# Reading the moving operand backwards, with high and low weights interleaved, in a hybrid encoder step

## The chip, the cores and the metric

The kernel runs on one core of one Trainium2 chip. The metric is the device time of that core in microseconds (us). The kernel before took 2157.94 us, the median of three runs (2157.59 to 2158.12).

## The reference

One inference step of a two-layer trunk in float32, on 1024 prompt frames and 32 sample frames of width 1024:

```python
def trunk(x, b_conv, b_h, c_conv, p):
    for l in range(DEPTH):                      # DEPTH = 2
        hn = rmsnorm(x, p['norm_mix_pre'][l])
        if l % 2 == 0:                          # gMLP spatial gating || RG-LRU, one in and one out projection
            m, v, bc, bh = mixer_even(hn, ...)  # 1024 -> 2048, 1024 -> 1024
        else:                                   # gated short convolution
            m, cc = mixer_odd(hn, ...)          # 1024 -> 3072, 1024 -> 1024
        x = x + rmsnorm(m, p['norm_mix_post'][l])
        hn = rmsnorm(x, p['norm_ffn_pre'][l])
        f = jnp.square(jax.nn.relu(hn @ p['mlp_up'][l])) @ p['mlp_down'][l]   # 1024 -> 4096 -> 1024
        x = x + rmsnorm(f, p['norm_ffn_post'][l])
```

Nearly all the arithmetic is in the projections. Everything else (norms, gates, convolutions, the scan) works on the 1056 x 1024 activations between them.

## The kernel before, in words

**Layout.** Channels lie on the 128 partitions and tokens along the free dimension. The 1056 tokens are cut into three tiles t = 0, 1, 2 of 352, and the 1024 channels into eight chunks k. Each activation is kept as a sum of two float32r tensors, a rounded high part and the low remainder: `x_hi`, `x_lo` for the residual stream's normed input, `h_hi`, `h_lo` for the inner activation. A chunk of x takes 4608 bytes in a partition and its tiles begin 1536 bytes apart. A chunk of h takes 4352 bytes and its tiles begin 1408 bytes apart.

**Products.** A *unit* is one 128-column panel of a weight matrix times one token tile. For each of the eight chunks k it issues three float32r matmuls of 128x128 by 128x352, high weights by high data (L698), high weights by low data (L699), low weights by high data (L700), and all 24 accumulate into one PSUM bank. There are 552 units; the first four are issued in another order (L716, L720, L729). Units rotate over six PSUM banks, so a unit may begin when the unit six before it has been read out.

**Weights.** A panel (512 KB) arrives by a DMA on SyncE's queue as raw float32. ScalarE writes the rounded high part (`high`, L876), VectorE writes the low part as raw minus high (`low`, L1183), and each raises a semaphore that the next engine waits for. 166 of the panels after the first four, and three of the first four, go to three *rotating places* p0, p1, p2. Each place is 8192 bytes of `w_all`: 4096 bytes of high weights, then 4096 of low weights, chunk after chunk of 512 bytes, and the raw weights land where the low ones will be written (`w_all_raw` is a second name of the same bytes). The other panels go to the place `s` in h, `x` in the gaps of `x_hi`, and `ha`, `hb` in h.

**Where things lie.** The tensors are laid one after another in a partition. `x_hi`, `x_lo`, `h_hi`, `h_lo` and `f` have sizes that are multiples of 1024 bytes; then 128 bytes are skipped, and `w_all` begins. So every chunk in a rotating place begins 128 bytes past a multiple of 512, counted from the start of `x_hi`. Tiles of x begin at multiples of 512; tiles 0 and 2 of h begin at multiples of 256, and tile 1 of h begins 128 bytes past a multiple of 256.

**Order.** The order on every engine is written out by hand. ScalarE's `high` of a panel stands at most six units before the panel's first use and VectorE's `low` one unit later. They stand among the reading out of PSUM (`evacuate`), the squares, the splits into high and low, and, between blocks, the norms, residual sums and splits of the new x. At the start, VectorE rounds the first half of the first panel (L1341), splits the first four chunks of x (L1248) and makes four low halves (L1330), each of 512 columns.

Of the kernel before, what the change touches and what calls it, by code (L numbers as in the profile page):

```python
# [13 lines left out]
P = 128  # L14
D = 1024
# [7 lines left out]
KC = D // P  # L23
# [27 lines left out]
F32 = mybir.dt.float32  # L51
F32R = mybir.dt.float32r
# [6 lines left out]
EVEN_COLS = [8, 9, 10, 11, 4, 5, 6, 7, 12, 13, 14, 15, 0, 1, 2, 3]  # L59
EVEN_KINDS = ["xb"] * 4 + ["v"] * 4 + ["gb"] * 4 + ["u"] * 4  # L60
ROTATING = ("p0", "p1", "p2")


def plan():
# [4 lines left out]
    units, loads, starts, outs, ups = [], [], [], [], []  # L69
    freed = {s: None for s in ROTATING}  # L70

    def oldest():
        return min(ROTATING, key=lambda s: -1 if freed[s] is None else freed[s])

# [19 lines left out]
    def tile_block(panels, src, slots):  # L94
        ls = []
        for (name, row, col, kind, m), (slot, free) in zip(panels, slots):
            if slot is None:
                slot = min((s for s in ROTATING if s not in [loads[l][3] for l in ls]),
                           key=lambda s: -1 if freed[s] is None else freed[s])
# [63 lines left out]
def build(nc, A, O):  # L163
# [27 lines left out]
    with ExitStack() as ctx:  # L191
        at_byte = [nc.sbuf_base + (-nc.sbuf_base) % 32]

        def place(name, shape, dt, offset=None):
            size = 4
            for n in shape[1:]:
                size *= n
            here = at_byte[0] if offset is None else offset
            if offset is None:
                at_byte[0] += size + (-size) % 32  # L200
            return nc.alloc_sbuf_tensor_at(name, shape, dt, offset=here)
# [6 lines left out]
        x_hi = place("x_hi", [P, KC * XS], F32R)  # L208
        at_x_lo = at_byte[0]
        x_lo = place("x_lo", [P, KC * XS], F32R)  # L210
# [6 lines left out]

        at_byte[0] += 128
        at_w = at_byte[0]
        w_all = place("w_all", [P, 6, D], F32R)  # L220
        w_all_raw = place("w_all_raw", [P, 6, D], F32, at_w)
        at_tmp = at_byte[0]
        tmp = [place(f"tmp{t}", [P, TT], F32) for t in range(3)]
        rstd = place("rstd", [P, TOK], F32)
# [64 lines left out]
        def tile_at(buf, t):  # L289
            return t * (TT + QUAD if buf.shape[1] == KC * XS else TT)  # L290

        def pt(buf, c, t):
            c0 = c * (buf.shape[1] // KC) + tile_at(buf, t)
            return buf[:, c0:c0 + TT]

        def part(buf, k0, k1, t, c0=0, c1=TT):
            return tiles3(buf)[:, k0:k1, tile_at(buf, t) + c0:tile_at(buf, t) + c1]
# [11 lines left out]
        def w_views(slot, l):  # L309
            if slot in ROTATING:  # L310
                s = ROTATING.index(slot)
                three = [w[:, i, :].rearrange("p (k n) -> p k n", k=KC)
                         for w, i in ((w_all, 2 * s), (w_all, 2 * s + 1), (w_all_raw, 2 * s + 1))]
            elif slot == "s":
                three = [w[:, i, :].rearrange("p (k n) -> p k n", k=KC)
                         for w, i in ((w_s, 0), (w_s, 1), (w_s_raw, 1))]
            elif slot == "x":
                three = [part(w, 0, KC, 2, c, c + P) for w, c in ((x_hi, 32), (x_hi, 32 + P), (x_hi_raw, 32 + P))]
            else:
                t = ("ha", "hb").index(slot)  # L320
                c = (32, 0)[t]
                if LOADS[l].first == START[2] + t:
                    three = [part(w, k, k + 4, t, c, c + 2 * P) for w, k in ((h_hi, 4), (h_hi, 0), (h_hi_raw, 0))]
                else:
                    three = [part(w, 4, 8, t, c, c + 2 * P) for w in (h_hi, h_lo, h_lo_raw)]
            return three

        W = [w_views(l.slot, i) for i, l in enumerate(LOADS)]

        def w_k(l, which, k):  # L330
            v = W[l][which]
            if LOADS[l].slot in ("ha", "hb"):
                return v[:, k // 2, (k % 2) * P:(k % 2) * P + P]
            return v[:, k, :]


        SLOTS = ROTATING + ("s", "x", "ha", "hb")
        fill = [sum(LOADS[j].slot == l.slot for j in range(i)) for i, l in enumerate(LOADS)]
# [5 lines left out]
        def bank(n):  # L344
            return ps[:, n % NB, 0:TT]
# [329 lines left out]
        def _(pe):  # L675
            EVEN_ORDER = (4, 5, 6, 7, 0, 1, 2, 3)
            IN_ORDER = tuple(range(KC))

            def unit(n):
                u = UNITS[n]  # L680
                X = u.src == "X"
                src = (x_hi, x_lo) if X else (h_hi, h_lo)
                order = EVEN_ORDER if u.kind == "eo" else IN_ORDER
                l, t = u.load, u.t
                pe.wait_ge(w_ready, l + 1)
                if n >= NB:
                    by_scalar = UNITS[n - NB].kind in SCALAR_OUT
                    pe.wait_ge(evac_a if by_scalar else evac_d, evac_no[n - NB] + 1)
                phase = START.index(max(s for s in START if s <= n))
                dst = bank(n)  # L690
                for i, k in enumerate(order):
                    if X and n - START[phase] in (0, 4, 8):
                        pe.wait_ge(x_ready, 24 * phase + 8 * t + k + 1)
                    if u.m == 0:
                        h_part(n, i)
                    hi, lo = pt(src[0], k, t), pt(src[1], k, t)
                    wh, wl = w_k(l, 0, k), w_k(l, 1, k)
                    nc.tensor.matmul(dst, wh, hi, start=(i == 0), stop=False)  # L698
                    nc.tensor.matmul(dst, wh, lo, start=False, stop=False)  # L699
                    last = nc.tensor.matmul(dst, wl, hi, start=False, stop=(i == KC - 1))  # L700
                    if i == KC - 1:
                        last.then_inc(pe_unit, 1)
                    between(n, i)

            def first_high(n, h):

                if h == 1:
                    pe.wait_ge(w_high, n + 1)
                elif n == 0:
                    pe.wait_ge(w_half, 1)  # L710
                else:
                    pe.wait_ge(w_halves, n)
                for k in range(4 * h, 4 * h + 4):
                    if n == 0:
                        pe.wait_ge(x_high, k + 1)
                    nc.tensor.matmul(bank(n), w_k(n, 0, k), pt(x_hi, k, 0), start=(k == 0), stop=False)  # L716
                for k in range(4 * h, 4 * h + 4):
                    if n == 0:
                        pe.wait_ge(x_ready, k + 1)
                    nc.tensor.matmul(bank(n), w_k(n, 0, k), pt(x_lo, k, 0), start=False, stop=False)  # L720

            def first_low(n, h):

                if h == 0:
                    pe.wait_ge(w_low, n + 1)
                else:
                    pe.wait_ge(w_ready, n + 1)
                for k in range(4 * h, 4 * h + 4):
                    last = nc.tensor.matmul(bank(n), w_k(n, 1, k), pt(x_hi, k, 0), start=False, stop=(k == KC - 1))  # L729
                if h == 1:  # L730
                    last.then_inc(pe_unit, 1)

            def h_part(n, i):

                kind, t = UNITS[n].kind, UNITS[n].t
                if kind in ("dn0", "dn", "dn3"):
                    done = index[n - 1 - t] + 1
                    if i == 0 and t == 0:
                        pe.wait_ge(h_ready, done - 3)
                    if i == KC - 1:  # L740
                        pe.wait_ge(h_ready, done - 2 + t)
                if kind == "oo":
                    if i == 0 and t == 0:
                        pe.wait_ge(y_ready, 21)
                    if i == KC - 1:
                        pe.wait_ge(y_ready, 22 + t)
                if kind == "eo":
                    if i == 0 and t == 0:
                        pe.wait_ge(mix_a, 12)
                    if i == 4 and t == 0:  # L750
                        pe.wait_ge(mix_a, 21)
                    if i == KC - 1:
                        pe.wait_ge(mix_a, 22 + t)
# [76 lines left out]
            def between(n, i):  # L830

                if n < START[1]:
                    if (n, i) in GATE_AT:
                        gate(*GATE_AT[n, i])
                    if (n, i) in VALUE_AT:
                        values_to_rows(*VALUE_AT[n, i])
                    if (n, i) in SPATIAL_AT:
                        spatial(SPATIAL_AT[n, i])
                if (n, i) in COL_AT:
                    col_sums(*COL_AT[n, i])  # L840
# [5 lines left out]
            for i, (n, h) in enumerate(turns):  # L846
                first_high(n, h)
                if i > 0:
                    first_low(*turns[i - 1])
            first_low(3, 1)  # L850
            for n in range(4, N_UNITS):
                unit(n)

            last = N_UNITS - 1
# [5 lines left out]
            n = NORM[3, "post", 2]  # L860
# [823 lines left out]
```

## Time and profile before

| | before |
|---|---|
| device time, median of three | 2157.94 us |
| span of the profiled execution, first to last instruction | 2155.1 us |
| device time of the profiled execution itself | not recorded beside its span |
| mean granted TensorE clock | 0.999 |
| matmuls (PE) busy | 2146.0 us, 100%, 13496 instructions |
| weight loads (PEld) busy | 2135.0 us, 99%, 13496 instructions |
| VectorE (DVE) busy | 908.0 us, 42% |
| ScalarE (ACT) busy | 652.9 us, 30% |
| GpSimd (POOL) busy | 100.1 us, 5% |
| DMA queues | 138.65 MB, mean 64 GB/s |

The times of a matmul and of a weight load in the profile include what overlaps the next one: matmuls are shown at about 322 ns although one begins every 158 ns or so. What counts for throughput is the distance from start to start. The median run stands 2.8 us above the profiled span; that is what lies around the span, and it is taken as constant.

### The profile page before, as it was taken

The numbers are of one execution on the slowest core, as the hardware profiler recorded it, in microseconds if no ns is written. First come the engines' busy times: TensorE is split into PE (matmuls) and PEld (weight loads), VectorE is DVE, ScalarE is ACT, GpSimd is POOL, SyncE is SP. The second block draws the span as 40 slices with busy tenths as digits, with TensorE's granted clock in tenths as the row PEclk, the third lists the DMA queues.
The fourth block names the chain that finished last, engine by engine and source line by source line (L and its number), as shares of the span: only waits on it lengthen the run. The fifth ranks groups of instructions, "written<-read, shape, count | busy, mean of one in ns | idle before, by whom it ended". The sixth has DMA issues, their size and how long they took to land.

```text
span 2155.1 us, 31488 instructions
## 1 busy us (share of the span) xinstructions
PE 2146.0 (100%) x13496; PEld 2135.0 (99%) x13496; DVE 908.0 (42%) x1414; ACT 652.9 (30%) x1105; POOL 100.1 (5%) x127
## 2 busy tenths in 40 slices
PE   9999999999999999999999999999999999999998
PEld 9999999999999999999999999999999999999998
DVE  8766367323322322334953333493223223322336
ACT  6673355202301310333511112453013103202332
POOL 2000000000000000000043231000000000000000
PEclk9999999999999999999999999999999999999999
DMA  5111422111111111141311114222111111111142
GB/s 165 35 41 40 139 88 72 50 40 49 50 42 47 49 50 40 49 135 44 120 50 47 43 50 139 67 84 59 42 48 50 49 40 50 50 42 48 50 140 81
DMA packets 208410, 138.65 MB, mean 64 GB/s; under 512 B 6000, under 2 KB 204784, under 8 KB 208272
## 3 DMA queue, kind: packets, MB, share of 16 engines
q1 hardware_dynamic: 207552, 135.51, 20.6%
q8 instruction: 107, 1.75, 0.3%
q10 hardware_dynamic: 720, 1.13, 0.1%
q14 instruction: 31, 0.25, 0.0%
HBM read 119.22 MB, written 17.40 MB: 63 GB/s over the span
## 4 chain that ended last, share of the span: by engine, by line
PE 99%; ACT 1%; DMA 0%; DVE 0%; issue 0%; DVEq 0%; ACTq 0%
PE ps L698 32%; PE ps L700 32%; PE ps L699 32%; PE ps L773 1%; PE ps L801 0%; PE ps L729 0%; PE ps L720 0%; DMA w_all_raw<-in_w_in_even_dram 0%; PE ps L716 0%; PE ps L784 0%; PE ps L760 0%; ACT L1074 0%; ACT L1030 0%; ACT lru L1030 0%; ACT lru L1032 0%; ACT gelu L1074 0%
## 5 line engine op out<-in xcount | busy, mean ns | idle before, releaser
L698 PE MATMUL ps<-x_hi,w_all 128*128 128x352 f32 x2304 | 747.0, 324 | 0.0
L700 PE MATMUL ps<-x_hi,w_all 128*128 128x352 f32 x2304 | 739.1, 321 | 0.0
L699 PE MATMUL ps<-x_lo,w_all 128*128 128x352 f32 x2304 | 739.1, 321 | 0.0
L698 PE MATMUL ps<-h_hi,w_all 128*128 128x352 f32 x1728 | 556.2, 322 | 0.0
L700 PE MATMUL ps<-h_hi,w_all 128*128 128x352 f32 x1728 | 555.2, 321 | 0.0
L699 PE MATMUL ps<-h_lo,w_all 128*128 128x352 f32 x1728 | 555.2, 321 | 0.0
L698 PEld LDWEIGHTS ps<-x_hi,w_all 128*128 128x128 f32 x2304 | 432.4, 188 | 2.7
L699 PEld LDWEIGHTS ps<-x_lo,w_all 128*128 128x128 f32 x2304 | 432.4, 188 | 2.2
L700 PEld LDWEIGHTS ps<-x_hi,w_all 128*128 128x128 f32 x2304 | 432.3, 188 | 0.0
L876 ACT CAST w_all<-w_all_raw 128x1024 fp32r<-128x1024 f32 x166 | 173.5, 1045 | 525.1 <-DMA w_all_raw<-in_mlp_down_dram 324.8
L698 PEld LDWEIGHTS ps<-h_hi,w_all 128*128 128x128 f32 x1728 | 324.5, 188 | 0.3 <-DVE h_lo L1452 0.3
L699 PEld LDWEIGHTS ps<-h_lo,w_all 128*128 128x128 f32 x1728 | 324.5, 188 | 0.0
L700 PEld LDWEIGHTS ps<-h_hi,w_all 128*128 128x128 f32 x1728 | 324.4, 188 | 0.0
L1286 DVE SCALAR_TENSOR_TENSOR tmp<-ps,rstd 128x352 f32<-128x352 f32 x192 | 100.3, 523 | 419.2 <-PE ps L700 419.0
L937 ACT ACTIVATE tmp<-tmp 128x352 f32<-128x352 f32 x192 | 95.7, 498 | 472.4 <-DVE tmp L1286 472.2
L1292 DVE TENSOR_TENSOR f<-ps,f 128x352 f32<-128x352 f32 x144 | 75.3, 523 | 358.6 <-PE ps L700 358.6
L1183 DVE TENSOR_TENSOR w_all<-w_all_raw,w_all 128x1024 fp32r<-128x1024 f32 x166 | 201.8, 1216 | 17.2 <-ACT w_all L876 17.2
L1266 DVE TENSOR_TENSOR h_lo<-tmp,h_hi 128x352 fp32r<-128x352 f32 x192 | 98.9, 515 | 2.3 <-ACT h_hi L939 2.3
L939 ACT CAST h_hi<-tmp 128x352 fp32r<-128x352 f32 x192 | 93.7, 488 | 6.1
L1289 DVE COPY f<-ps 128x352 f32<-128x352 f32 x48 | 25.2, 525 | 138.0 <-PE ps L700 138.0
L698 PE MATMUL ps<-h_hi,x_hi 128*128 128x352 f32 x192 | 61.7, 321 | 0.0
L700 PE MATMUL ps<-h_hi,x_hi 128*128 128x352 f32 x192 | 61.7, 321 | 0.0
(201 smaller groups left out, 1416.0 us busy)
## 6 DMA issues: line engine op xcount, KB each, us to landing
w_all_raw<-in_mlp_up_dram SPq DMA_DIRECT2D x60, 512.0 KB, 3.9
w_all_raw<-in_mlp_down_dram SPq DMA_DIRECT2D x60, 512.0 KB, 3.8
x_save<-f SPq DMA_DIRECT2D x9, 1408.0 KB, 6.0
x_old<-x_save SPq DMA_DIRECT2D x9, 1408.0 KB, 11.5
w_all_raw<-in_c_w_in_dram SPq DMA_DIRECT2D x22, 512.0 KB, 3.7
w_all_raw<-in_w_in_even_dram SPq DMA_DIRECT2D x12, 512.0 KB, 3.6
x_old<-in_x_cols_dram SPq DMA_DIRECT2D x3, 1408.0 KB, 12.8
w_all_raw<-in_w_out_even_dram SPq DMA_DIRECT2D x6, 512.0 KB, 3.8
```

The source lines that it names most:

```text
L698: nc.tensor.matmul(dst, wh, hi, start=(i == 0), stop=False)
L699: nc.tensor.matmul(dst, wh, lo, start=False, stop=False)
L700: last = nc.tensor.matmul(dst, wl, hi, start=False, stop=(i == KC - 1))
L773: nc.tensor.matmul(ps[:, M0, 0:LT], gate_w[:, g, j, :], xc[j % 2][:, t * LT:(t + 1) * LT], start=True, stop=True).then_inc(gate_pe, 1)
L876: nc.scalar.copy(W[l][0], W[l][2]).then_inc(w_high, 1)
L937: nc.scalar.activation(tmp[n % 3][:, :], tmp[n % 3][:, :], ACT.Square).then_inc(h_sq, 1)
L939: nc.scalar.copy(pt(h_hi, u.m, u.t), tmp[n % 3][:, :]).then_inc(h_high, 1)
L1183: nc.vector.tensor_tensor(lo, raw, hi.bitcast(F32), ALU.subtract).then_inc(w_ready, 1)
L1266: nc.vector.tensor_tensor(pt(h_lo, u.m, u.t), tmp[n % 3][:, :], pt(h_hi, u.m, u.t).bitcast(F32), ALU.subtract).then_inc(h_ready, 1)
L1286: ins = nc.vector.scalar_tensor_tensor(tmp[n % 3][:, :], bank(n), 0.0, scale, ALU.max, ALU.mult)
L1289: ins = nc.vector.tensor_copy(pt(f, m, t), bank(n))
L1292: ins = nc.vector.tensor_tensor(pt(f, m, t), bank(n), pt(f, m, t), ALU.add)
```

## The change

All the projection matmuls now go through a helper `product`, which gives the moving operand and the result in reversed column order: the last of the 352 columns is read and written first. The result lies in PSUM as before.

In the rotating places the high and the low weights of a column lie side by side (4 bytes of high, 4 of low), so a chunk of 128 columns takes 1024 bytes and one weight load reads every second word. The three places begin at 0, 8192 and 16384 bytes, moved further by 0, 16 and 96 bytes. Raw weights have a tensor of their own, `w_raw`, of 3 x 4096 bytes. To make room, the DMA scratch reservation is set to 2048 bytes, which moves all tensors in a partition together. The places `s`, `x`, `ha`, `hb` keep their layout. No wait, queue or order is changed.

```diff
+W_SHIFT = (0, 4, 24)
+WS = len(ROTATING) * 2 * D + 32
...
-        w_all = place("w_all", [P, 6, D], F32R)
-        w_all_raw = place("w_all_raw", [P, 6, D], F32, at_w)
+        w_all = place("w_all", [P, WS], F32R)
+        w_raw = place("w_raw", [P, len(ROTATING), D], F32)
...
             if slot in ROTATING:
                 s = ROTATING.index(slot)
-                three = [w[:, i, :].rearrange("p (k n) -> p k n", k=KC)
-                         for w, i in ((w_all, 2 * s), (w_all, 2 * s + 1), (w_all_raw, 2 * s + 1))]
+                at = s * 2 * D + W_SHIFT[s]
+                pairs = w_all[:, at:at + 2 * D].rearrange("p (k n two) -> p two k n", two=2, n=P)
+                three = [pairs[:, 0], pairs[:, 1], w_raw[:, s, :].rearrange("p (k n) -> p k n", k=KC)]
...
+            def product(out, w, x, start, stop):
+
+                return nc.tensor.matmul(out[:, ::-1], w, x[:, ::-1], start=start, stop=stop)
...
-                    nc.tensor.matmul(dst, wh, hi, start=(i == 0), stop=False)
-                    nc.tensor.matmul(dst, wh, lo, start=False, stop=False)
-                    last = nc.tensor.matmul(dst, wl, hi, start=False, stop=(i == KC - 1))
+                    product(dst, wh, hi, i == 0, False)
+                    product(dst, wh, lo, False, False)
+                    last = product(dst, wl, hi, False, i == KC - 1)
...
-    nc = _bacc.Bacc("TRN2", target_bir_lowering=False, num_devices=1)
+    nc = _bacc.Bacc("TRN2", target_bir_lowering=False, num_devices=1, dynamic_dma_scratch_size=2048)
```

The matmuls of the first four units are changed in the same way.

## Rows read from the trace of the kernel before

**Rows 1.** The page: busy time by engine, granted clock, shares of the ending chain

```profile
PE 2146.0 (100%) x13496; PEld 2135.0 (99%) x13496; DVE 908.0 (42%) x1414; ACT 652.9 (30%) x1105; POOL 100.1 (5%) x127
...
PEclk9999999999999999999999999999999999999999
...
PE 99%; ACT 1%; DMA 0%; DVE 0%; issue 0%; DVEq 0%; ACTq 0%
```

**Rows 2.** Groups: line, engine, operation, tensors, shape, count | busy, mean ns | idle before

```profile
L698 PE MATMUL ps<-x_hi,w_all 128*128 128x352 f32 x2304 | 747.0, 324 | 0.0
L698 PE MATMUL ps<-h_hi,w_all 128*128 128x352 f32 x1728 | 556.2, 322 | 0.0
...
L876 ACT CAST w_all<-w_all_raw 128x1024 fp32r<-128x1024 f32 x166 | 173.5, 1045 | 525.1 <-DMA w_all_raw<-in_mlp_down_dram 324.8
L1183 DVE TENSOR_TENSOR w_all<-w_all_raw,w_all 128x1024 fp32r<-128x1024 f32 x166 | 201.8, 1216 | 17.2 <-ACT w_all L876 17.2
L1398 DVE TENSOR_TENSOR_SCAN mixed<-lru,lru 128x1024 f32<-128x1024 f32 x4 | 9.2, 2292 | 0.4
```

**Rows 3.** Busy time in stretches: stretch, its length, each engine's busy time (instructions)

```profile
0.00:50.00 50.00, 48.26 (x275) 45.36 (x276) 40.54 (x71) 30.71 (x48) 12.35 (x39) 1.00 0.53 172
500.00:1000.00 500.00, 500.00 (x3155) 500.00 (x3154) 156.22 (x261) 126.65 (x213) 0.00 (x0) 1.00 0.19 56
```

**Rows 4.** Timeline, TensorE, three matmuls in a row: start us, length us

```profile
1000.40 0.32 PE L698 MATMUL ps<-h_hi,w_all 128*128 128x352 f32 x1
1000.56 0.32 PE L699 MATMUL ps<-h_lo,w_all 128*128 128x352 f32 x1
1000.71 0.32 PE L700 MATMUL ps<-h_hi,w_all 128*128 128x352 f32 x1
```

**Rows 5.** Timeline, TensorE: first matmuls of units on h's tiles 0, 1, 2, 0

```profile
598.74 0.32 PE L698 MATMUL ps<-h_hi,w_all 128*128 128x352 f32 x1
...
602.54 0.32 PE L698 MATMUL ps<-h_hi,w_all 128*128 128x352 f32 x1
...
606.38 0.32 PE L698 MATMUL ps<-h_hi,w_all 128*128 128x352 f32 x1
...
610.18 0.32 PE L698 MATMUL ps<-h_hi,w_all 128*128 128x352 f32 x1
```

**Rows 6.** Timeline, TensorE: float32 passes of 352 columns before the first unit

```profile
4.35 0.76 PE L810 MATMUL ps<-rstd 128*128 128x352 f32 x2
...
5.54 0.46 PE L810 MATMUL ps<-rstd 128*128 128x352 f32 x1
```

**Rows 7.** Timeline, matmuls and weight loads after a wait, next load not held back

```profile
6.33 0.43 PE L716 MATMUL ps<-x_hi,w_all 128*128 128x352 f32 x1 [0.33 <-DVE w_all L1341]
...
6.44 0.19 PEld L716 LDWEIGHTS ps<-x_hi,w_all 128*128 128x128 f32 x1
...
6.59 0.53 PE L716 MATMUL ps<-x_hi,w_all 128*128 128x352 f32 x2
```

**Rows 8.** Timeline, the same after a wait, next load held back

```profile
8.31 0.42 PE L720 MATMUL ps<-x_lo,w_all 128*128 128x352 f32 x1
...
8.56 0.19 PEld L716 LDWEIGHTS ps<-x_hi,w_all 128*128 128x128 f32 x1
...
8.57 0.42 PE L716 MATMUL ps<-x_hi,w_all 128*128 128x352 f32 x1
```

**Rows 9.** Timeline, a product while a 32-column weight load runs

```profile
83.92 0.32 PE L700 MATMUL ps<-x_hi,w_all 128*128 128x352 f32 x1
...
83.92 0.10 PEld L787 LDWEIGHTS ps<-ident,gelu 128*32 128x32 f32 x1
...
84.08 0.27 PE L787 MATMUL ps<-ident,gelu 128*32 128x128 f32 x1
```

**Rows 10.** Timeline, a low panel of VectorE and the unit that uses it

```profile
1054.24 1.18 DVE L1183 TENSOR_TENSOR w_all<-w_all_raw,w_all 128x1024 fp32r<-128x1024 f32 x1
...
1056.60 0.32 PE L698 MATMUL ps<-x_hi,w_all 128*128 128x352 f32 x1
```

**Rows 11.** Timeline, VectorE at the start

```profile
5.85 0.43 DVE L1341 CAST w_all<-w_all_raw 128x512 fp32r<-128x512 f32 x1 [4.62 <-DMA w_all_raw<-in_w_in_even_dram]
6.19 2.06 DVE L1248 SCALAR_TENSOR_TENSOR x_lo<-f,vecs,x_hi 128x352 fp32r<-128x352 f32 x4
```

More of the change, by code:

```diff
@@ L715, in first_high @@
                         pe.wait_ge(x_high, k + 1)
-                    nc.tensor.matmul(bank(n), w_k(n, 0, k), pt(x_hi, k, 0), start=(k == 0), stop=False)
+                    product(bank(n), w_k(n, 0, k), pt(x_hi, k, 0), k == 0, False)
                 for k in range(4 * h, 4 * h + 4):
@@ L719, in first_high @@
                         pe.wait_ge(x_ready, k + 1)
-                    nc.tensor.matmul(bank(n), w_k(n, 0, k), pt(x_lo, k, 0), start=False, stop=False)
+                    product(bank(n), w_k(n, 0, k), pt(x_lo, k, 0), False, False)
             def first_low(n, h):
@@ L728, in first_low @@
                 for k in range(4 * h, 4 * h + 4):
-                    last = nc.tensor.matmul(bank(n), w_k(n, 1, k), pt(x_hi, k, 0), start=False, stop=(k == KC - 1))
+                    last = product(bank(n), w_k(n, 1, k), pt(x_hi, k, 0), False, k == KC - 1)
                 if h == 1:
```

## The prediction

> **What bounds the kernel now.** I read the page first, then the groups, then stretches of busy time, then the timeline at single instructions. The page says that TensorE is busy over the whole span, at the full of its two clock levels (2.4 GHz) in every slice, and the chain that ended last is 99% TensorE [rows 1]. No other engine is near it: VectorE 42%, ScalarE 30%. So only two things can move the time: the distance between matmul starts, or a new wait of TensorE.
>
> The groups show what the matmuls are: products of 128x352 in float32r, of which 4 x 24 belong to the first units and 548 x 24 = 13,152 to the rest, 13,248 in all. Those with weights in `w_all` are 3 x (2304 + 1728) = 12,096 on L698 to L700 [rows 2], and 3 x 24 = 72 in the first units, so 12,168 read a rotating place and 1,080 another one. The busy mean of 322 ns is no cost, since matmuls overlap; the stretch from 500 to 1000 us gives the cost: 3155 starts in 500.00 us, 158.5 ns each [rows 3]. At 2.4 GHz, 352 columns at one a cycle are 146.7 ns. So 11.8 ns of each matmul, 7.4%, is not columns, and 12,168 x 11.8 ns = 144 us is all that the change could ever reach.
>
> How much of that is unavoidable? The nearest row is a float32 pass of 352 columns, at two cycles a column: four of them begin in 5.54 - 4.35 = 1.19 us, about 297 ns each where the columns take 293.3 [rows 6]. That leaves some 3 to 4 ns between passes, and a float32r product would stand at about 150 ns with no more loss than that. 158.5 has some 8.5 ns more.
>
> Does this excess depend on addresses? A unit of 24 matmuls on h's tile 0 takes 602.54 - 598.74 = 3.80 us, on tile 1 3.84, on tile 2 3.80 [rows 5]: 158.3, 160.0, 158.3 ns a matmul with the same weights. From the layout, weights of a rotating place and tile 1 begin at the same place modulo 256 bytes, and the other tiles 128 bytes apart. So reading weights and reading moving data do disturb each other by address, and 1.7 ns of it shows. Singly, starts stand 0.16 and then 0.15 us apart [rows 4]: the disturbance varies from one matmul to the next, and the short ones are near 155 ns.
>
> Does it come from the weight load at all? After a wait the next load starts 6.44 - 6.33 = 0.11 us later, once the first has been read, and the second product starts 0.15 us after that, at 0.26 [rows 7]. In the other case the next load is held back until 8.56, when the product before it is practically over, and the distance is again 8.57 - 8.31 = 0.26 us [rows 8]. And where only 32 columns of weights are loaded beside a product, it takes 84.08 - 83.92 = 0.16 us [rows 9]. Within the 10 ns of these rows, a product without a weight load beside it is hardly shorter. This speaks against the load as the cause of all 8.5 ns, and for a cost of the float32r stream itself.
>
> **The change part by part.** *Reversed moving columns and results.* No row of before reads or writes backwards. Lower bound: it takes away the whole excess, 150 ns a product. Upper bound: backwards runs at the rate of the float32 passes, 297 ns. I take no cost and no gain by itself, since 352 columns backwards touch the same words.
>
> A rule of the Trainium skill speaks against this part: "PSUM — Partial Sum Buffer", section Specifications, says that any non-contiguous access pattern slows matmuls significantly, because PSUM's lines are 8 bytes. A step of -1 has the same pairs in the other order; if it counted as non-contiguous, the rule would put the kernel with the backwards rival below, towards its far end of 3990 us. No trace here shows which holds.
>
> *Weights side by side.* A load now reads every second word, so it walks 8 bytes for each weight, twice as far as before. In 0.11 us the load walks 1024 bytes, and the moving stream, at 352 x 4 bytes in 147 ns, walks 1024 bytes in 107 ns: both now move at the same pace. No row shows in which order the load takes its columns. If it is last to first, the two now walk side by side and keep their distance, where before they crossed; if it is first to last, they cross faster than before. With a kept distance, each product should look like the undisturbed ones. For these I take the short distance of the timeline, 155 ns [rows 4], between no change (158.5) and the bound of 150. That is 3.5 ns x 12,168 = 43 us less. The 1,080 products of other places I leave as they are; at 3.5 ns they would add at most 4 us. The offsets of 16 and 96 bytes decide where the kept distance lies: if it is bad, tile 1's row says what that costs, 160 ns, or +1.5 x 12,168 = +18 us.
>
> *ScalarE's and VectorE's panels.* `high` now writes, and `low` reads and writes, every second word: 166 x 1045 ns and 166 x 1216 ns today [rows 2]. No row has a step of two. Bounds: no change, or the slowest VectorE group of 1024 columns, 2292 ns, that is +1.08 us each, +179 us of VectorE in all; ScalarE's bound is the same sum, at most +179 us. Neither is on the chain: 908 + 179 is 50% of the span, and readouts have six banks of 3.8 us each. What they can hit are the tight places between blocks. At 1054.24 a `low` ends at 1055.42 and its unit starts at 1056.60, 1.2 us later [rows 10]; behind that instruction on VectorE the readouts and the squares' sums queue. Two such panels in a row at +0.8 each (nearer the upper end, since every stream but one is strided) would be 0.4 us late. The trace has about six such places with 1.2 to 2.3 us to spare, so 0 to 6 us, and I take 2.
>
> The Trainium skill's "Vector Engine (DVE) Microarchitecture Reference", section 5.2, measured streams without adjacent pairs at about 1.7 to 2.5 ns a column against 1.05. By that, 1024 columns would gain 0.7 to 1.5 us each, and the 2 us would become up to 6 or 8. No row here shows it.
>
> *The start.* L1341 (0.43 us for 512 columns) is on the path, and the four splits behind it too [rows 11]. A strided write may cost 0 to 0.5 us there; I take 0.5. The four low halves behind have 1.9 us per turn of TensorE.
>
> *Raw weights apart, scratch.* Nothing: the same DMAs to another place behind the same waits; 64 GB/s is far from a bound, and the scratch only moves everything together.
>
> **Sum.** Against the profiled execution: 2155.1 - 43 + 2 + 0.5 = 2114.6 us of span. The median of the runs is 2.8 us above the span, so 2157.9 - 40.5 = 2117 us.
>
> **The rivals.**
> *The whole excess goes.* The 8.5 ns are all crossing of the two streams. For it: the excess depends on addresses, and float32 passes at half the pace lose only 3 to 4 ns. Against: the held-back and the 32-column load [rows 8, 9]. 8.5 x 12,168 = 103 us, plus the 2.5: 2057 us.
> *It does nothing.* The excess is the stream's own, and the 1.7 ns of tile 1 moves from one tile to another: 2153 to 2162 us. For it: rows 7 against 8.
> *Slower by place or feed.* The streams now lie as on tile 1 at all times (+18 us), or `low` at 2.3 us makes units wait; it decides once the delay of two panels passes 1.2 us: 2165 to 2180 us.
> *Slower by backwards reading or writing.* Each product pays for the reversed order. At 1 ns a product it would be +13 us; at the full bound, 297 ns, +138.5 x 13,248 = +1835 us, 3990 us. It decides from 3.5 ns a product up. For it only that TensorE's stream has no slack; against it that every word is touched once, as before.
>
> **How the numbers follow.** My forecast, 10 to 70 us saved, has 0.33; the whole excess 0.20; a small gain of 4 to 10 us 0.10; nothing 0.13; slower by place or feed 0.10; slower by backwards access 0.14. Faster: 0.63, same (within 0.2%, 4.3 us, about what a measurement of this kernel can tell) 0.13, slower 0.24. The range goes from 2045, below the whole-excess case with the other places' 4 us and a margin for its 150 ns, up to 2178, which takes in the case of place and feed. Left out are most of the backwards case and little below. The likeliest case's own range is 2088 to 2148.
>
> **What would show it.** In the stretch from 500 to 1000 us the count of matmuls should rise from 3155 to about 3225 (150 ns: 3333; 160 ns: 3125). Units on tile 1 should be as long as on tiles 0 and 2, except where an offset differs; units of p0, p1 and p2 may differ from one another. `low` should be longer than 1216 ns, `high` than 1045, with a few tenths of idle TensorE at block boundaries. TensorE stays busy 99%. I am wrong if the distance is unchanged, if matmuls at all places lengthen alike (backwards access), or if TensorE's idle time before L698 grows to tens of us.

## The result, and the profile after

| | before | after |
|---|---|---|
| device time, median | 2158.03 us (4 runs, 2157.59 to 2159.05) | 2176.68 us (4 runs, 2176.47 to 2176.76) |
| ratio to before, 95% interval | | 1.0086 (1.0072 to 1.0100) |
| span of the profiled execution | 2155.1 us | 2174.9 us |
| busy VectorE, ScalarE | 908.0, 652.9 us | 913.8, 673.2 us |

The kernel after is 18.7 us, 0.86%, slower. Faster was forecast (2117 us). The forecast's range went up to 2178 us only to take in the rival of place and feed; that the measured time lies just inside it is luck, since neither turned out to be the cause.

The busy times of the kernel after:

```profile
PE 2166.4 (100%) x13496; PEld 2155.5 (99%) x13496; DVE 913.8 (42%) x1414; ACT 673.2 (31%) x1105; POOL 95.0 (4%) x127
```

The middle stretch of the kernel after, columns as in [rows 3]; the 1.00 behind the busy times is the granted clock:

```profile
500.00:1000.00 500.00, 500.00 (x3124) 500.00 (x3123) 153.05 (x255) 128.17 (x206) 0.00 (x0) 1.00 0.20 57
```

TensorE is as busy as before at the same clock, 1.00 of 2.4 GHz [rows 1, 3]: no new wait, more time in each product. 3124 starts in 500 us are 160.1 ns a product, against 3155 and 158.5 [rows 3]. All projections now go through one line, L684. The timeline of the kernel after shows the units on h's tiles 0 and 1. Each row begins with the last product of the unit before, so 24 products lie between one row and the next:

```profile
603.21 0.48 PE L684 MATMUL ps<-h_hi,w_all 128*128 128x352 f32 x2
...
607.05 0.48 PE L684 MATMUL ps<-h_hi,w_all 128*128 128x352 f32 x2
...
610.94 0.49 PE L684 MATMUL ps<-h_hi,w_all 128*128 128x352 f32 x2
```

3.84 and 3.89 us for tiles 0 and 1, where it was 3.80 and 3.84 [rows 5]. These are units of p2, whose tile 1 of h is the one bad case left among the rotating places. Over the 548 units after the first four, the starts in the two traces lie 2120.8 and 2140.4 us apart, first to last. That is 19.6 of the span's 19.8 us; the rest is the start. (The medians differ by 1.1 us less than the spans, since the profiled execution of before has its span 2.9 us below the median, that of after 1.8.)

The groups of the kernel after, weight loads of a rotating place and of another one, then the two panel operations:

```profile
L684 PEld LDWEIGHTS ps<-h_hi,w_all 128*128 128x128 f32 x3456 | 613.4, 194 | 0.3 <-DVE h_lo L1459 0.3
L684 PEld LDWEIGHTS ps<-h_hi,x_hi 128*128 128x128 f32 x384 | 67.4, 188 | 0.0
...
L883 ACT CAST w_all<-w_raw 128x1024 fp32r<-128x1024 f32 x166 | 193.7, 1167 | 531.3 <-DMA w_raw<-in_mlp_down_dram 325.3 <-DMA w_raw<-in_mlp_up_dram 124.9 <-DMA w_raw<-in_c_w_in_dram 59.8
...
L1190 DVE TENSOR_TENSOR w_all<-w_raw,w_all 128x1024 fp32r<-128x1024 f32 x166 | 207.2, 1248 | 18.8 <-ACT w_all L883 18.8
```

`high` is the rounding to the high part on ScalarE, `low` the subtraction on VectorE. A load with a step of two is shown 6 ns longer (194 against 188). `high` grew from 1045 to 1167 ns, `low` only from 1216 to 1248 [rows 2].

### The profile page after: what moved, and what is told of

Read it like the earlier page. It is cut to its first block, busy times and chain, and to the rows that moved or that the text cites. A ratio compares the mean times of both kernels' runs of the same rounds, so it can differ in the third digit from the quotient of the medians.

```text
span 2174.9 us, 31488 instructions
## 1 busy us (share of the span) xinstructions
PE 2166.4 (100%) x13496; PEld 2155.5 (99%) x13496; DVE 913.8 (42%) x1414; ACT 673.2 (31%) x1105; POOL 95.0 (4%) x127
## 4 chain that ended last, share of the span: by engine, by line
PE 60%; issue 38%; POOL 0%; DVE 0%; DMA 0%; ACT 0%; DVEq 0%; ACTq 0%; POOLq 0%
PE ps L684 59%; PE ps L780 1%; PE ps L808 0%; DMA w_raw<-in_w_in_even_dram 0%; PE ps L791 0%; DVE cy L1510 0%; POOL cy L664 0%; POOL h_lo L667 0%; DVE x_lo L1255 0%; POOL row_rstd L673 0%; PE ps L767 0%; ACT h_hi L1154 0%; DVE x_old L1633 0%; PE ps L812 0%; DVEq L193 0%
## 5 line engine op out<-in xcount | busy, mean ns | idle before, releaser
L684 PE MATMUL ps<-x_hi,w_all 128*128 128x352 f32 x4656 | 1133.7, 326 | 0.0
L684 PE MATMUL ps<-h_hi,w_all 128*128 128x352 f32 x3456 | 837.2, 324 | 0.0
L684 PEld LDWEIGHTS ps<-x_hi,w_all 128*128 128x128 f32 x4656 | 825.4, 194 | 3.1 <-ACT w_all L992 0.2
L684 PE MATMUL ps<-x_lo,w_all 128*128 128x352 f32 x2328 | 751.7, 324 | 0.1
L684 PEld LDWEIGHTS ps<-h_hi,w_all 128*128 128x128 f32 x3456 | 613.4, 194 | 0.3 <-DVE h_lo L1459 0.3
L684 PE MATMUL ps<-h_lo,w_all 128*128 128x352 f32 x1728 | 559.5, 324 | 0.0
L684 PEld LDWEIGHTS ps<-x_lo,w_all 128*128 128x128 f32 x2328 | 450.7, 194 | 2.5 <-DVE x_lo L1255 0.3
L883 ACT CAST w_all<-w_raw 128x1024 fp32r<-128x1024 f32 x166 | 193.7, 1167 | 531.3 <-DMA w_raw<-in_mlp_down_dram 325.3
L684 PEld LDWEIGHTS ps<-h_lo,w_all 128*128 128x128 f32 x1728 | 335.7, 194 | 0.0
L1190 DVE TENSOR_TENSOR w_all<-w_raw,w_all 128x1024 fp32r<-128x1024 f32 x166 | 207.2, 1248 | 18.8 <-ACT w_all L883 18.8
L684 PE MATMUL ps<-h_hi,x_hi 128*128 128x352 f32 x384 | 95.3, 325 | 0.0
L684 PEld LDWEIGHTS ps<-h_hi,x_hi 128*128 128x128 f32 x384 | 67.4, 188 | 0.0
L684 PE MATMUL ps<-h_lo,x_hi 128*128 128x352 f32 x192 | 62.3, 325 | 0.0
L1268 DVE TENSOR_TENSOR x_hi_raw<-x_hi_raw,tmp 128x352 f32<-128x352 f32 x56 | 29.2, 521 | 68.4 <-ACT tmp L937 67.5
```

What stands on the lines that cost most here:

```text
L684: return nc.tensor.matmul(out[:, ::-1], w, x[:, ::-1], start=start, stop=stop)
L883: nc.scalar.copy(W[l][0], W[l][2]).then_inc(w_high, 1)
L1190: nc.vector.tensor_tensor(lo, raw, hi.bitcast(F32), ALU.subtract).then_inc(w_ready, 1)
L1268: nc.vector.tensor_tensor(dst, dst, sq, ALU.add).then_inc(f_acc, 1)
```

## The experiments

In this table the last six columns are the mean distance from one product's start to the next, in ns, worked out from the starts of all products in each trace: the rotating places, chunks two to seven of each unit, by the source (x or h) and its tile. Distances of over 175 ns, where a short matmul of another kind lies between or is just over, are left out. Ratios have 95% intervals; a time without one is a single run (before: four).

| kernel | us | ratio to before | x 0 | x 1 | x 2 | h 0 | h 1 | h 2 |
|---|---|---|---|---|---|---|---|---|
| before | 2158.0 | | 158.4 | 158.6 | 158.6 | 158.4 | 160.0 | 158.4 |
| after | 2176.7 | 1.0086 (1.0072 to 1.0100) | 160.0 | 160.0 | 160.0 | 160.0 | 160.7 | 160.0 |
| e1 reversed only | 2187.1 | 1.0134 (1.0117 to 1.0151) | 161.0 | 161.0 | 161.0 | 160.1 | 162.2 | 160.2 |
| e2 interleaved only | 2185.4 | 1.0127 (1.0112 to 1.0142) | 160.8 | 160.8 | 160.9 | 161.3 | 161.1 | 160.8 |
| e3 after, no shift | 2175.4 | 1.0079 (1.0064 to 1.0094) | 160.0 | 160.0 | 160.0 | 160.0 | 160.0 | 160.0 |
| e4 after, result forward | 2176.6 | | 160.0 | 160.0 | 160.0 | 160.0 | 160.7 | 160.0 |
| e5 reversed, moved | 2182.9 | | 160.7 | 160.7 | 160.7 | 160.7 | 160.0 | 160.7 |
| e6 after, moved | 2175.5 | | 160.0 | 160.0 | 160.0 | 160.0 | 160.0 | 160.0 |
| f1 forward, moved | 2181.4 | 1.0109 (1.0092 to 1.0126) | 160.7 | 160.7 | 160.7 | 160.7 | 160.0 | 160.8 |
| e8 narrow loads, forward | 2153.1 | | 158.6 | 159.2 | 157.8 | 158.4 | 157.8 | 157.9 |
| e9 narrow, reversed | 2178.7 | | 160.9 | 160.0 | 160.0 | 160.1 | 161.6 | 160.0 |
| e10 narrow, interleaved | 2173.4 | | 160.8 | 159.7 | 159.6 | 160.8 | 159.9 | 159.9 |
| e11 narrow, after | 2174.4 | | 160.0 | 160.0 | 160.0 | 160.0 | 160.1 | 160.0 |
| e7 fewer columns, forward | 2011.5 | | 158.4 | 146.7 | 133.3 | 158.3 | 146.5 | 133.3 |
| e12 fewer columns, after | 2017.9 | | 160.0 | 146.8 | 131.9 | 160.0 | 147.8 | 131.9 |

**e1, e2: each half alone.** In e1 the old layout of the weights stays:

```diff
-                return nc.tensor.matmul(out, w, x, start=start, stop=stop)
+                return nc.tensor.matmul(out[:, ::-1], w, x[:, ::-1], start=start, stop=stop)
```

> The kernel before with only the moving columns and results reversed. If backwards access alone causes the loss: 160.0 ns a product in all places and 2174 to 2178 us. If the interleaved weight loads (194 ns shown against 188) cause it: unchanged, 2156 to 2160 us. If only the two together do (both streams at one pace): 155 to 159 ns here, 2120 to 2160 us.

In e2 the kernel after has that line turned back.

> The kernel after with moving columns and results forward again; interleaved weights stay. Backwards access as the cause: 158.3 ns again, 2157 to 2162 us. Weight loads as the cause: 160 ns in p0, p1, p2 and 158.3 in x, ha, hb, 2172 to 2178 us. The two together as the cause: below 160 ns, 2155 to 2165 us.

The same stretch of e1 and, below it, of e2:

```profile
500.00:1000.00 500.00, 500.00 (x3121) 500.00 (x3120) 151.98 (x255) 122.26 (x205) 0.00 (x0) 1.00 0.19 56
```

```profile
500.00:1000.00 500.00, 500.00 (x3108) 500.00 (x3107) 150.62 (x251) 125.56 (x204) 0.00 (x0) 1.00 0.19 56
```

Neither expectation names this outcome: each half alone costs more than both together, +29.1 and +27.4 us against +18.7. In e2 the loss is nearly all in the rotating places; products from `ha` and `hb`, forward and contiguous there, are at 158.3 ns in the units that no other matmul interrupts. It also differs by rotating place, and the places differ by their shift: on x's tiles p0 has 160.1 ns, p1 160.0 and p2 162.4 to 162.5. In e1 it is everywhere, `ha` and `hb` at 162.2. The 161.0 of e1 on x is a mean of two kinds of units: in each rotating place some 16 units stand at 160.0 ns and 12 to 14 at 162.2, with weights and data at the same addresses.

**e3: the shifts.**

```diff
-W_SHIFT = (0, 4, 24)
+W_SHIFT = (0, 0, 0)
```

> The kernel after with the three places shifted by 0, 0, 0 bytes instead of 0, 16, 96. If the place of the weights decides: p1 and p2 become as p0, the 162.2 ns of p2 on h's tile 1 go to 160.0, 1.3 us less (2175 us). If the shifts had helped p1 and p2: p1, p2 above 160 ns, 2180 us or more.

1.3 us less than after, as the first theory had it, all of it from p2 on h's tile 1. The shifts of 16 and 96 bytes do nothing useful.

**e4: the direction of writing.**

```diff
-                return nc.tensor.matmul(out[:, ::-1], w, x[:, ::-1], start=start, stop=stop)
+                return nc.tensor.matmul(out, w, x[:, ::-1], start=start, stop=stop)
```

> The kernel after with the results written forward while the moving columns are read backwards; the token columns of each tile come out permuted, so the values are not the reference's. If writing PSUM backwards costs anything: 1.5 ns a product less, 2157 us. If only reading decides: 160.0 ns as after, 2176 us.

```profile
500.00:1000.00 500.00, 500.00 (x3124) 500.00 (x3123) 153.06 (x256) 128.15 (x206) 0.00 (x0) 1.00 0.19 57
```

3124 starts, exactly as in the kernel after. Writing PSUM backwards costs nothing that can be seen beside backward reading; what there is comes from reading.

**e5, e6, f1: other places.** e5 is e1 with the places moved by 64, 128, 192 bytes, e6 the kernel after with those shifts, f1 the kernel before with 32, 64, 192 bytes. The core of e5 and f1 (e5's numbers):

```diff
+W_SHIFT = (16, 32, 48)
...
-                         for w, i in ((w_all, 2 * s), (w_all, 2 * s + 1), (w_all_raw, 2 * s + 1))]
+                at = [i * D + W_SHIFT[s] for i in (2 * s, 2 * s + 1)]
+                three = [w[:, c:c + D].rearrange("p (k n) -> p k n", k=KC)
+                         for w, c in ((w_all, at[0]), (w_all, at[1]), (w_all_raw, at[1]))]
```

> Reversed moving columns with contiguous weights, the three places moved by 64, 128, 192 bytes. A tile read backwards begins 1404 bytes later, that is some 128 bytes on modulo 256. If only the place where the two streams meet decides, p1 (moved by 128) returns to 158.3 ns on x's tiles, and 160 on h's tile 1; p0 and p2 lie between. If reading backwards itself costs, every place stays at 160 ns or more, 2175 us or more.

> The kernel after with shifts of 64, 128, 192 bytes instead of 0, 16, 96. If the kept distance of two streams of one pace decides, some place is clear of the other stream and falls to 155 ns or less, another rises above 162. If pairs and backwards reading hold the products at 160.0 whatever the distance, all three places stay within 0.5 ns of 160 on x's tiles, 2174 to 2180 us.

> Forward columns and contiguous weights as before, the three places moved by 32, 64, 192 bytes (160, 192 and 64 past a multiple of 256). If only meeting at one place modulo 256 costs: 158.3 ns for all tiles in p1 and p2, tile 1 of h included, 2 us less than before in all. If the present place is the only good one: 160 ns in p1, p2 also on x, 2165 us or more. If a place can free the product of all disturbance: 155 ns somewhere.

Reversed and contiguous (e5), p0 and p2 stand at 160.0 ns on x and p1, the one that should have come back to 158.3, at 162.2. Backwards, no place that was tried is below 160.0. Forward and contiguous (f1), p1 and p2 have 160.0 ns on every tile, p0 162.0 to 162.3 on all but h's tile 1, where it has 160.0: of the places tried, the one that the kernel before has (128 past a multiple of 256) is the only one at 158.3. The smaller scratch reservation, which f1 has and before has not, is not the cause: in f1 products from place `x`, whose weights did not move, are still at 158.3 ns on h's tiles 0 and 2. Interleaved and reversed (e6), it is 160.0 whatever the place:

```profile
500.00:1000.00 500.00, 500.00 (x3126) 500.00 (x3125) 153.22 (x256) 128.26 (x208) 0.00 (x0) 1.00 0.19 57
```

The place is not the whole story. Two units of f1 take their weights from `ha`, at the same addresses, times tile 2 of x. The first product of each and the first of the next unit:

```profile
345.24 0.33 PE L684 MATMUL ps<-x_hi,h_hi 128*128 128x352 f32 x1
...
349.24 0.33 PE L684 MATMUL ps<-x_hi,h_hi 128*128 128x352 f32 x1
```

```profile
1458.18 0.32 PE L684 MATMUL ps<-x_hi,h_hi 128*128 128x352 f32 x1
...
1461.99 0.32 PE L684 MATMUL ps<-x_hi,h_hi 128*128 128x352 f32 x1
```

4.00 against 3.81 us for the same 24 products. The starts show why: the first unit runs at a steady 166 to 167 ns, the second in the cycle 155, 159, 157 or 158, 161 or 162. f1 falls into the slow rhythm within five products of two short matmuls of the norms, which stand at 320.2 us in the middle of a `hb` unit that had run at 158.3 ns until then. So a stream settles in one of a few rhythms (with full loads of contiguous weights, means such as 158.3, 160.0, 162.2 or 166.7 ns forwards, 160.0 or 162.2 backwards), and how it was entered counts beside the places. What chooses the rhythm was not tested. A mean of the table can be a mixture of such rhythms. In before, two uninterrupted units of the rotating places stand at 166.7 ns.

**e8, e9, e10, e11: hardly any weight load beside the product.** The same edit in four kernels: forward and contiguous (e8), reversed (e9), interleaved (e10), both (e11, shown as e8):

```diff
+            def product(out, w, x, start, stop, t=0):
+                m = P if start or stop else (128, 64, 32)[t]
+                return nc.tensor.matmul(out[0:m], w[:, 0:m], x, start=start, stop=stop)
```

> The kernel before where 22 of 24 products of a unit load 128, 64, 32 weight columns on tiles 0, 1, 2 (on tiles 1 and 2 the upper output channels are summed incompletely). If the excess of 8.5 ns is weight load against moving stream: about 158.3, 154, 151 ns on x's tiles. If it is the stream's own: all within 1 ns of 158.3.

> Reversed columns, contiguous weights, and the narrowed loads of e8 (128, 64, 32 weight columns on tiles 0, 1, 2; upper output channels summed incompletely). Forward, the narrow loads gave 157.9 ns on tile 2. If backwards reading costs by itself: 160 ns or more on tile 2 too. If it costs only by meeting the weight load: about 158 on tile 2, 161 on tile 0.

> Forward columns, interleaved weights, narrowed loads of 128, 64, 32 columns (upper output channels summed incompletely). If the interleaved load disturbs by the lines it reads: the loss of 1.8 to 4 ns shrinks with the number of columns, about 158 ns on tile 2. If each load with a step of two costs a fixed amount: 160 to 162.5 on tile 2 as on tile 0.

> The kernel after with narrowed loads of 128, 64, 32 columns on tiles 0, 1, 2 (upper output channels summed incompletely). If side by side at one pace has already removed what the load disturbs, and 160.0 ns is the backward stream's own distance: 160.0 on all tiles, within 0.3 ns. If a disturbance by the load is still in the 160.0: tile 2 falls to 158 or less.

In e8 loads of 128 columns are shown at 188 ns, of 64 at 134, and those of 32:

```profile
L681 PEld LDWEIGHTS ps<-h_hi,w_all 128*32 128x32 f32 x1008 | 108.8, 108 | 49.4
```

Of 188 ns shown, 80 are gone at 32 columns, and the product hardly gains. The timeline of e8, one unit on h's tile 2 (row to row, 24 products):

```profile
604.82 0.48 PE L681 MATMUL ps<-h_hi,w_all 128*128 128x352 f32 x2
...
608.62 0.48 PE L681 MATMUL ps<-h_hi,w_all 128*128 128x352 f32 x2
```

The same of e9, reversed:

```profile
610.65 0.49 PE L681 MATMUL ps<-h_hi,w_all 128*128 128x352 f32 x2
...
614.49 0.48 PE L681 MATMUL ps<-h_hi,w_all 128*128 128x352 f32 x2
```

The same of e11, reversed and interleaved:

```profile
610.18 0.48 PE L684 MATMUL ps<-h_hi,w_all 128*128 128x352 f32 x2
...
614.02 0.49 PE L684 MATMUL ps<-h_hi,w_all 128*128 128x352 f32 x2
```

3.80, 3.84 and 3.84 us. With a quarter of the load, a forward product takes 157.8 to 157.9 ns, 0.5 to 0.8 less than with all of it (with half of it, x's tile 1 has 159.2, 0.6 more); a backward one 160.0; and the kernel after keeps its 160.0 on every tile. These are no mixtures: with 32 columns loaded, all 151 uninterrupted units of the rotating places on tile 2 stand at 157.7 to 158.0 ns in e8 and at 159.9 to 160.0 in e9. So in the kernel after the load disturbs next to nothing (in p2 on h's tile 1, 162.2 ns becomes 160.2), and 160.0 is the distance of a backward product of 352 columns at the alignments of these tiles. e10 lies between its two theories: on tile 2 of x, p0 has 160.7 (160.1 in e2), p1 158.2 (160.0) and p2 160.0 (162.5). The interleaved load disturbs a forward product, partly by its columns.

**e7, e12: fewer columns.**

```diff
+            def product(out, w, x, start, stop, t=0):
+                n = TT if start or stop else (352, 320, 288)[t]
+                return nc.tensor.matmul(out[:, 0:n], w, x[:, 0:n], start=start, stop=stop)
```

> The kernel before where 22 of 24 products of a unit take 352, 320, 288 columns on tiles 0, 1, 2 (the last columns of tiles 1 and 2 are summed incompletely). Measures what the 11.7 ns above the columns are. A fixed cost of each product: 13.3 ns less for each 32 columns, 158.3, 145.0, 131.7 ns on x's tiles. A share of the stream: 14.4 less, 158.3, 143.9, 129.5. Bound by the weight load: no product under 158.

e12 is the same on the kernel after, with both slices reversed.

> The kernel after where 22 of 24 products take 352, 320, 288 columns on tiles 0, 1, 2, backwards (the last columns of tiles 1 and 2 summed incompletely). Forward, x's tiles gave 158.4, 146.9, 133.7 ns. If reading backwards costs a fixed amount a product: about 160.0, 148.5, 135.4. If it costs by the column: the distance to forward shrinks, to 1.4 at 288. If only the length of 352 is unlucky: 146.7 and 133.3, as forward.

The timelines on h's tile 2 (22 products of 288 columns and two of 352 from row to row), e7 and below it e12:

```profile
568.98 0.48 PE L681 MATMUL ps<-h_hi,w_all 128*128 128x352 f32 x2
...
572.23 0.48 PE L681 MATMUL ps<-h_hi,w_all 128*128 128x352 f32 x2
```

```profile
572.09 0.49 PE L684 MATMUL ps<-h_hi,w_all 128*128 128x352 f32 x2
...
575.30 0.48 PE L684 MATMUL ps<-h_hi,w_all 128*128 128x352 f32 x2
```

3.25 us forward, 3.21 us backward, for a unit of p2. Taking the columns off at 2.4 GHz (146.7, 133.3, 120.0 ns), a forward product on x's tiles has 11.8, 13.3 and 13.3 ns beside them, a backward one 13.3, 13.5 and 11.9. From 320 to 288 columns a forward product becomes 13.3 ns shorter, which is just its 32 columns; from 352 to 320 it becomes 11.7 shorter. So the cost is one for each product and not for each column, and it moves by a nanosecond or two with length and direction. At 320 columns backwards is as fast as forwards on x (146.8 and 146.7). At 288 it is 1.4 ns faster on average, and there the place counts again: 131.1 ns in p1 and p2, 133.3 in p0. So 352 columns forwards, at 11.8, is the cheap case among the forward ones, and backwards the product of 352 has the 13.3 ns that 320 and 288 have forwards.

## Why the prediction was wrong

**What bounds the kernel: right.** The change acts only by the distance between starts, and 19.6 of 19.8 us of the span lie there.

**The step that failed: "For these I take the short distance of the timeline, 155 ns".** I took the short distances of [rows 4] for undisturbed products and the long ones for disturbed ones. e8 shows a forward product with little load beside it at 157.9 ns on average: short and long distances (155 to 162 ns) still take turns there, and only their mean means something. As far as a quarter of the load shows it (none at all was not run), the load's disturbance in the kernel before is then 0.5 to 0.8 ns, and 2.2 on h's tile 1, where half the load was enough to lose it. The prediction had the warning in hand: with the next load held back, and with a load of 32 columns, the distance stayed the same [rows 8, 9]. It set these rows against the 103 us rival and not against its own 43 us.

**The step behind it: "I take no cost and no gain by itself".** Reading 352 columns backwards costs 160.0 ns against 157.9 with little load beside it (e9 against e8, tile 2), about 2.1 ns a product. Times 13,248 that is 28 us. This term was set at zero between its bounds, because the same words are read, and it is what turned the sign.

**The mechanism of the kept distance: it fits the runs, for nothing.** With both streams at one pace, the effect of place is nearly gone: at 352 columns five of the six shifts tried (0, 16, 64, 96, 128 and 192 bytes) give 160.0 ns on every tile from the rotating places (after, e3, e6), only p2 with 96 bytes has 162.2 on tile 1 of h. Reversed alone has means from 160.1 to 162.2, interleaved alone from 160.0 to 162.5, and both together 160.0. That is why two changes of +29 and +27 us come to +19. But what it takes away is a nanosecond of disturbance that the reversal has first added to. The order in which a load takes its columns was not measured; that reversed and interleaved go well together fits last to first, but does not show it.

**The sum by its terms.** Against before, products of the rotating places lose 1.4 to 1.6 ns on x and on h's tiles 0 and 2, and 0.7 on tile 1 of h; the panels' feed nothing; the start 0.24 us. Over all 13,152 products of the later units the mean goes from 158.7 to 160.2 ns: 1.47 x 13,152 = 19.3 us, against 19.6 measured between first and last start.

**Panels: direction right, size too large.** `low` was given +0.8 us and took +0.03, `high` took +0.12 of up to +1.08. The `low` of [rows 10] is done 1.3 us before its unit, not later than before, because TensorE is slower. The Trainium skill's "Vector Engine (DVE) Microarchitecture Reference", section 5.2, measured 1.7 to 2.5 ns a column for streams without adjacent pairs. Here one source and the result step by two words, so they have no adjacent pairs either, and yet 1024 columns grew by 32 ns only; where the two differ the measurement decides, and it gives a step of two no such price.

**The rivals.** "Slower by place or feed" named the time (2165 to 2180 us) and 160 ns a product, but not the cause: shifts are worth 1.3 us (e3) and no feed came late. That it hit the time is luck. "Slower by backwards reading" is the right one, and the 1 ns a product that it reckoned with was half of the measured 2.1; the writing that it named beside the reading costs nothing (e4). The Trainium skill's "PSUM — Partial Sum Buffer", section Specifications, says that any non-contiguous pattern slows matmuls significantly. For a result written with a step of -1 this case does not bear it out: e4 has 3124 starts against 3124. "The whole excess goes" is refuted: 11.8 ns above the columns stay at 11.2 with a quarter of the load (157.9 - 146.7), and e7 shows them as a fixed cost of the product. "It does nothing" had the bound right, that the excess is the stream's own.

**What stays open.** What the 12 to 13 ns of each float32r product consist of, when four float32 passes of 352 columns lose only about 3 each [rows 6], and why it is less for 352 columns forwards than for 320. What decides which rhythm a stream settles in, and why a step of -1 costs at 352 columns and not at 320: only tiles that begin at multiples of 128 bytes were read. e12 against e7 compares kernels that differ in the weights' layout too; by e11 the load no longer matters at 352 columns, but at 288 p0 stands apart, and reversed products of 288 columns with contiguous weights were not run. For h's tile 1 the three places of f1 gave the same 160.0 ns; whether it would gain from weights 128 bytes further on was not tried: at 1.6 ns for its 1,920 products (1,728 in rotating places, 192 in `x`) it would be an estimated 3.1 us. No kernel that does all the work beat the kernel before.

## What to carry to other kernels

A distance between starts that alternates (155, 159, 157, 162) has to be read as a mean over its whole cycle; its short members are no price for anything. Before a layout is changed to spare TensorE a collision with its weight loads, load fewer weight columns on some tiles and look whether the products come closer: one run (e8) shows the size of the gain. And look at single units before trusting a mean: the same unit can run in a fast or a slow rhythm (3.81 and 4.00 us in f1). Here, 157.9 ns everywhere in place of 158.7 would be 11 us ((158.7 - 157.9) x 13,152), against the 43 us forecast. And a move with two parts that only work together (equal pace and equal direction) needs the price of each part alone, since the first part has to earn back what the second costs.

## What the runs showed of the hardware that was not expected

- A float32r product of 128x352 starts every 158 to 160 ns, 11.2 to 13.3 above its columns, with 128 or with 32 weight columns loaded beside it (before, after, e8, e9); at 320 and 288 columns it is 13.3 above them forwards (e7).
- The direction in which the moving operand is read changes the distance: 157.9 against 160.0 ns at 352 columns (e8, e9), 133.3 against 131.9 at 288 (e7, e12, means over three places). The direction in which PSUM is written does not (e4).
- Weights and moving data disturb each other by where they lie: forward and contiguous 158.3, 160.0 or 162 ns by place (before, f1, on x), forward and interleaved up to 162.5 (e2).
- The same products on the same addresses can run in more than one steady rhythm: 158.5 or 166.7 ns (f1, weights in `ha`, x's tile 2), 160.0 or 162.2 (e1, x's tiles). A short matmul in between can switch it (f1 at 320.2 us).
- A weight load with a step of two words is shown at 194 ns against 188, a ScalarE write of 1024 such words at 1167 (1126 in e2) against 1045, a VectorE subtraction with them at 1248 against 1216.
